# Expert stage of a decoder step: token rows gathered by index, with and without the slots that hold no token

## The reference, cut to what matters

```
xb = x_pad[idx]                                   # the token rows of one block
h = jax.nn.silu(xb @ w_gate[e]) * (xb @ w_up[e])  # 1024 -> 512
return h @ w_down[e]                              # 512 -> 1024
...
y = segment_sum(yb * row_w[:, None], row_tok, ...)  # each token: the weighted sum of its two rows
```

## Time and profile before

| what | value |
|---|---|
| time, median of 3 runs | 1741.79 us (1738.52 to 1743.24) |
| the profiled execution's own time | 1736.78 us |
| its span, first to last instruction | 1735.0 us |
| TensorE busy in the span | 1493.1 us, 86% |
| VectorE, ScalarE, GpSimd busy | 990.6, 733.1, 237.2 us |
| DMA over the span | 347.56 MB, 200 GB/s in the mean |

### The profile page before, as it was taken

The page is one execution under the profiler, slowest core; times in us unless marked ns, Lnnn a source line. Parts: engine busy times, 40 slices in busy tenths (PEclk is TensorE's granted clock), DMA queues, the critical chain, the costliest instruction groups (busy, mean ns, idle before and its releaser), DMA issues. The chain is left out here.

```text
span 1735.0 us, 22122 instructions
## 1 busy us (share of the span) xinstructions
PE 1493.1 (86%) x8308; PEld 1267.3 (73%) x8308; DVE 990.6 (57%) x1299; ACT 733.1 (42%) x835; POOL 237.2 (14%) x245
## 2 busy tenths in 40 slices
PE   6799999789999996797469974999999999999970
PEld 5799999779999996787358863666666667666650
DVE  5222311145555553746245655888788888878855
ACT  7121121134444442210021111777777777776742
POOL 4200000001111111121010001112112111111104
PEclk9899999899999998899689985999999999999985
DMA  3322228323332312735744125999999999999828
GB/s 137 116 92 69 69 69 258 129 76 111 102 94 91 92 50 65 183 91 110 159 150 183 42 76 207 333 382 383 368 378 384 372 372 385 376 370 384 322 76 308
DMA packets 144429, 347.56 MB, mean 200 GB/s; under 512 B 22468, under 2 KB 100676, under 8 KB 118696
## 3 DMA queue, kind: packets, MB, share of 16 engines
q1 hardware_dynamic: 134632, 312.38, 51.6%
q0 software_dynamic: 6160, 21.89, 4.0%
q10 hardware_dynamic: 3584, 12.58, 1.8%
HBM read 292.91 MB, written 54.89 MB: 200 GB/s over the span
## 5 line engine op out<-in xcount | busy, mean ns | idle before, releaser
L449 PE MATMUL pj<-w_hi,f_hi 128*128 128x352 f32 (+3 forms) x576 | 189.1, 328 | 14.1 <-ACTq L171 14.1
L450 PE MATMUL pj<-w_lo,f_hi 128*128 128x352 f32 (+3 forms) x576 | 188.5, 327 | 0.0
L451 PE MATMUL pj<-w_hi,f_lo 128*128 128x352 f32 (+3 forms) x576 | 188.4, 327 | 0.0
L2005 DVE TENSOR_TENSOR e_w_lo<-mixed,e_w_hi 128x2048 fp32r<-128x2048 f32 x64 | 145.8, 2297 | 43.0 <-ACT e_w_hi L1938 43.0
L2005 DVE TENSOR_TENSOR e_w_lo<-w_out,e_w_hi 128x2048 fp32r<-128x2048 f32 x64 | 143.5, 2283 | 0.0
L840 PE MATMUL gate_banks<-f_hi,wg_hi 128*128 128x364 f32 (+1 forms) x384 | 130.9, 341 | 10.3 <-PEq L93 7.6
L1938 ACT CAST e_w_hi<-mixed 128x2048 fp32r<-128x2048 f32 x64 | 118.8, 1906 | 39.5 <-PEq L93 21.2
L841 PE MATMUL gate_banks<-f_lo,wg_hi 128*128 128x364 f32 (+1 forms) x384 | 127.2, 331 | 0.0
L842 PE MATMUL gate_banks<-f_hi,wg_lo 128*128 128x364 f32 (+1 forms) x384 | 127.1, 331 | 0.0
L1938 ACT CAST e_w_hi<-w_out 128x2048 fp32r<-128x2048 f32 x64 | 121.7, 1902 | 1.7 <-PE e_up L2075 1.7
L2073 PE MATMUL e_gate<-e_w_hi,e_x_hi 128*96 128x512 f32 x256 | 105.5, 412 | 17.9 <-DVE e_w_lo L2005 17.9
(11 more groups left out here) (465 smaller groups left out, 3456.4 us busy)
## 6 DMA issues: line engine op xcount, KB each, us to landing
w_out<-in_w_down_e SPq DMA_DIRECT2D x64, 1024.0 KB, 8.1
mixed<-in_w_gate_e SPq DMA_DIRECT2D x32, 1024.0 KB, 6.9
mixed<-in_w_up_e SPq DMA_DIRECT2D x32, 1024.0 KB, 8.3
w_gate<-in_w_gate_e SPq DMA_DIRECT2D x32, 1024.0 KB, 7.1
w_up<-in_w_up_e SPq DMA_DIRECT2D x32, 1024.0 KB, 8.6
expert_rows<-e_y_rows ACTq DMA_DIRECT2D x32, 384.0 KB, 8.0
proj<-mixed SPq DMA_DIRECT2D x8, 1408.0 KB, 6.1
proj_tile<-proj SPq DMA_DIRECT2D x8, 1408.0 KB, 6.2
```

Source lines behind the costliest of these rows:

```text
L449: pe.matmul(banks[b][:r, :w], hi, w_hi[v][:, k, 0:w], start=(k == 0), stop=False)
L450: pe.matmul(banks[b][:r, :w], hi, w_lo[v][:, k, 0:w], start=False, stop=False)
L451: ins = pe.matmul(banks[b][:r, :w], lo, w_hi[v][:, k, 0:w], start=False, stop=(k == KD - 1))
L2005: dve.tensor_tensor(lo(i, u, j), raw(i, u, j), hi(i, step, j).bitcast(F32), ALU.subtract).then_inc(lo_ready[i], 1)
```

## The change

The token numbers in `tok` are lowered by 4096, and 4096 is added again when the table leaves PSUM. A slot with a token keeps its number; one without a token, whose sum is 0, now gets 4096, which is no row of `xh2` (1088 rows). The gathers of the expert stage are issued with a bound of 1087 and told that an index past it is no error: such a row is to be passed over, and what stood in that row of `xb[u]` stays. So that never-written memory isn't read, VectorE clears both `xb` buffers at the stage's start, and GpSimd waits for that before it starts each of the first two gathers.

```diff
+NO_TOKEN = 4096
...
-                c.link(pool.iota(iota_i[:, 0:NT + 1], pattern=[[P, NT + 1]], base=0, channel_multiplier=1))
+                c.link(pool.iota(iota_i[:, 0:NT + 1], pattern=[[P, NT + 1]], base=-NO_TOKEN, channel_multiplier=1))
...
-                L(dve.tensor_copy(R.token_of[:, 0:MAXB], LG[:SLOTS, 0:MAXB]))
+                L(dve.tensor_scalar(R.token_of[:, 0:MAXB], LG[:SLOTS, 0:MAXB], float(NO_TOKEN), None, ALU.add))
...
-                    pool.indirect_dma_start(xb[u][:], None, a["xh2"], bass.IndirectOffsetOnAxis(ap=idx[u][:, 0:1], axis=0)).then_inc(xb_loaded[u], 16)
+                    pool.indirect_dma_start(xb[u][:], None, a["xh2"], bass.IndirectOffsetOnAxis(ap=idx[u][:, 0:1], axis=0),
+                                            bounds_check=T - 1, oob_is_err=False).then_inc(xb_loaded[u], 16)
                 for u in range(2):
+                    pool.wait_ge(s["x_rows_zero"], u + 1)
                     gather(u, u)
...
+                for u in range(2):
+                    dve.memset(xb[u][:], 0.0).then_inc(s["x_rows_zero"], 1)
                 for j in range(2):
                     split(GATE, 0, 0, j, 0)
                 x_split(0, 0)
```

More of the change, by code:

```diff
@@ L1846, in experts @@
         ring = [sb(f"w_hi{n}", [P, PIECE], F32R) for n in range(4)]
-        names = """idx_ready idx_seen all_stored xT_full x_hi_ready x_lo_ready silu_ready h_ready hT_full h_hi_ready h_lo_ready
+        names = """x_rows_zero idx_ready idx_seen all_stored xT_full x_hi_ready x_lo_ready silu_ready h_ready hT_full h_hi_ready h_lo_ready
             y_act""".split()
```

## The result

The changed kernel takes 1746.79 us (median of 20 runs, 1742.69 to 1752.14), the kernel before, in 20 runs beside it, 1743.29 us. The ratio is 1.0022, 95% interval 1.0012 to 1.0031: 2.1 to 5.4 us slower, 3.8 us in the middle. That is inside the forecast range and inside the 0.3% that I called no change, but it is a loss and about three times the forecast's +1.2 us. The kernel before had a median of 1741.79 us in the three runs that the forecast started from, so 1.5 us of the distance between 1743.0 and 1746.79 us are scatter of its own. The profiled execution took 1743.65 us, its span is 1741.9 us.

A forecast was written before the change was run, and what follows sets the result against it. TensorE's matmuls plus a 0.58 us ScalarE/VectorE chain per block bound it, not DMA; 0 (bytes) + 0 (addition) + 1.3 (clears and wait) - 0.1 (smaller gathers) + 0 (bound) = +1.2 us on 1741.79: 1743.0 us, range 1738 to 1747.5.

The forecast's parts named there:

- What bounds the stage: Expert stage: a block's period is its matmuls plus 0.58 us of a ScalarE and VectorE chain; DMA has slack.
- The bytes: GpSimd's queue in the expert stage: 4.06 MB fewer, covered in the loop, worth 0 us; 5168 packets expected.
- rival 3: Gathers: an index past the bound moves a row all the same, 6160 packets stay; 1743.1 us, 5%.
- The addition in route: End of route: a cast out of PSUM becomes an addition with a cast; 0, between -0.1 and 0.1 us.
- The clears and the wait: Expert stage's start: the wait pushes gather 0's issue into VectorE's lo part, making turn(1) late; +1.3 us.
- The upper bound: Stage's start: bounded issues 2.1 us longer each, counted twice, make turn(1) 4.0 us late instead of 1.3.
- The wait's own bounds: Stage's start: the term for clears and wait was put between 0 and 1.5 us, 1.3 taken.
- the forecast's own range: Whole time: bounds 0 to 4.0, less 0.3, with run scatter -3.3 to +1.5 us; 1738.5 to 1747.
- The bound's price: Gather issues: the bound lengthens each by 0 to 2.1 us, covered in the loop; taken as 0.
- rival 2: Bounded issues go a slow way in GpSimd, handling each passed row, exposed by the first two gathers; 1749.6 us, 9%.
- Smaller gathers: Stage's start: the two gathers TensorE waits for land sooner with fewer packets; 0.1 us taken from the path.
- The page against the trace: Stage's start: by the skill's inference gather 0 would end at 1067.9, cost 0; the trace's 2.13 us speaks against it.

The follow-up runs named there:

- e5: Changed kernel with 8192 added to the table, so every gather passes over all its rows; ratio to the kernel before 1.0012 (0.9997 to 1.0027).
- e1: Changed kernel with table and unbounded gathers as before the change, clears and wait kept; ratio to the kernel before 1.0037 (1.0020 to 1.0055).
- e8: Changed kernel with VectorE's second weight lo part moved behind the lo part of block 0's token rows; ratio to the kernel before 1.0025 (1.0013 to 1.0036).
- e2: Changed kernel with the bound kept, table as before, no clears and no wait; ratio to the kernel before 1.0001 (0.9988 to 1.0013).
- e6: Kernel before, VectorE's first weight lo part waiting for block 0's rows, the second behind these rows' lo part; ratio to the kernel before 1.0004.
- e4: Changed kernel with VectorE's first two weight lo parts waiting for a semaphore GpSimd raises behind each gather's issue; ratio to the kernel before 1.0018.

## Why the prediction was right, and where it was off

- **What bounds the stage:** right. The period and TensorE's wait are unchanged, and e5 shows it to the point where no row is moved.
- **The bytes:** 4.06 MB and 0 us, right. The packets were wrong: a passed row leaves a small one, and none disappears. So 6160 packets, which I had named as the sign of rival 3, came about although the bytes are gone; the count doesn't tell the two apart, the MB do.
- **The addition in route:** 0.21 us as the cast; right.
- **The clears and the wait:** this is the step that was mis-sized, 1.3 us as the term had it, 4.2 measured. The mechanism was right: the clears push GpSimd's issue into VectorE's lo part, where it is held, and e1 puts the whole loss there. Wrong was the sentence that the issue would end 0.8 us behind the first lo part. I had read that from the row of 2.13 us, which lay in the second of the pair, where no other lo part followed. Held by both, issue 0 ended 7.80 us after the stage's start where I had 5.0, and turn(1), which I had 1.3 us late, came 4.2 us late behind it. e8 is the case that I had computed, with one lo part in the way: there turn(1) comes 2.0 us late, so the second lo part makes 2.2 of the 4.2 us, and my sum was 0.7 us short even for one. A smaller error: VectorE begins 0.33 us behind ScalarE, so the first lo part came 0.3 us late where I said 0.1 us of cover.
- **The upper bound** of 4.0 us for this start came out of the bound's price, not of the wait; that the measured loss lies near it is luck. The wait's own bounds, 0 to 1.5, didn't hold the 4.2. The lower end of the forecast's own range was added up wrongly by 0.3 us (1741.79 - 0.3 - 3.3 is 1738.2, not 1738.5); the range went down to 1738, so nothing hangs on it.
- **The bound's price:** taken as 0; e2 has gate 0.2 us late and a ratio of 1.0001 (0.9988 to 1.0013). Its issues in the loop do take 3.0 us, the value of my upper row, under a cover of 33 us. They do so in e2 too, where no row is passed over, so this isn't the slow handling of passed rows of rival 2.
- **Smaller gathers:** I took 0.1 us; in the changed kernel turn(0) starts 3.25 us behind the issue's end, as before, so 0. Only with no row at all does it shorten, to 1.1 us (e5).
- **The page against the trace:** by the inference in the Trainium skill (SBUF — State Buffer, Who interferes with whom), that the making of descriptors isn't kept out by such an instruction of VectorE, I had worked out a cost of 0. e6 and e8 speak against that use of it: issues of 2.13 and 5.27 us fall to 0.93 and 3.07 when only VectorE's instructions are moved. Whether it is the making of descriptors that is held, or the issue's reading of its indices (`e_idx` lies in SBUF), no run here separates.

## What to carry to other kernels

A transfer that nobody waits for gave nothing here when it got smaller (e5: 8.9 MB further, the loop unchanged), however full the DMA looked; look for the slack between landing and first use. What the edit adds to make it safe (here a clear and a wait, 0.9 us) is paid where the pipeline fills and nothing covers it, and it can be paid several times over when it moves a GpSimd instruction into a run of VectorE instructions. Before delaying a GpSimd DMA, see how many VectorE instructions of the kind that held it here (subtractions with both inputs in SBUF) follow each other from there, and reckon with all of them.

## What the runs showed of the hardware that I had not expected

- An indirect DMA's issue that begins 0.2 to 0.6 us inside the first of two adjacent VectorE subtractions of 2.2 us is held through both (5.27, 5.30, 4.64 us instead of 1.2 to 1.3); inside a single one, to 1.15 us behind its end (3.07). One that begins inside the subtraction of 0.96 us with an input in PSUM isn't held (0.93).
- A row passed over by its bound still makes a packet, under 512 B. A gather whose rows are all passed over lands 1.1 us behind its issue at the stage's start, where whole ones take 3.1 to 3.4 us.
- A GpSimd semaphore increment queued behind an indirect DMA went off before that instruction ran (e4: VectorE, which waited for it, began at 1069.99; the issue began at 1070.16).
